# One hybrid decoder layer on one core: the small matmuls of the head turns gathered into fewer groups

## The reference, cut to what matters

```python
q = (rms_norm(c_q) @ w_uq);  kv = (rms_norm(c_kv) @ w_ukv)      # 16 heads, 128 + 64 and 128 + 128 wide
s = (q_nope @ k_nope.T + q_rope @ k_rope.T) * scale             # causal mask, softmax
mla_out = softmax(s) @ v
st = associative_scan(a, B u);   y = Re(C st) + D u             # state-space branch, per group
ssm_out = glu(gelu(y) @ w_glu)
h = layer_norm(alpha * h + (g_ssm * ssm_out + g_mla * mla_out) @ w_out)
h = layer_norm(alpha * h + (silu(h @ w_gate) * (h @ w_up)) @ w_down)
```

## Time and profile before

| what | value |
|---|---|
| median of three runs | 1333.01 us |
| the profiled execution's own time | 1332.76 us |
| its span in the profile | 1330.6 us |
| PE busy | 1320.0 us |
| PE weight loads busy | 1249.1 us |
| DVE busy | 835.4 us |
| ACT busy | 648.7 us |
| granted TensorE clock, mean | 1.00 of full speed |

### The profile page before, as it was taken

How to read it: one execution, slowest core, us unless ns; L and a number is a source line. 1 busy time by engine, 2 the same in 40 slices (tenths; PEclk the granted TensorE clock), 3 DMA queues, 4 the chain that set the end, 5 groups by cost and what they waited for, 6 DMA issues and landing times.

```text
span 1330.6 us, 28260 instructions
## 1 busy us (share of the span) xinstructions
PE 1320.0 (99%) x11052; PEld 1249.1 (94%) x11052; DVE 835.4 (63%) x1232; ACT 648.7 (49%) x910; POOL 23.1 (2%) x50
## 2 busy tenths in 40 slices
PE   9999999999999999999999999999999999999998
PEld 8999999999999998879999999999999998888896
DVE  6787868687786776577555655555555555545545
ACT  5566556474656454365444444444444453434332
POOL 0022000000001000000000000000000000000000
PEclk9999999999999999999999999999999999999999
DMA  8656545545476775754656666666666676556562
GB/s 287 206 190 191 161 157 159 154 141 183 135 192 184 250 246 197 241 169 149 200 190 190 191 195 194 191 190 197 195 190 192 215 236 193 191 173 216 175 207 98
DMA packets 79774, 253.21 MB, mean 190 GB/s; under 512 B 16544, under 2 KB 17504, under 8 KB 79584
## 3 DMA queue, kind: packets, MB, share of 16 engines
q1 hardware_dynamic: 78304, 251.69, 59.8%
q0 software_dynamic: 1408, 0.63, 0.2%
HBM read 248.08 MB, written 2.10 MB: 188 GB/s over the span
## 4 chain that ended last, share of the span: by engine, by line
PE 96%; DVE 2%; ACT 1%; DMA 1%; issue 0%; SPq 0%; DVEq 0%
PE ps L895 22%; PE ps L896 22%; PE ps L897 22%; PE ps L907 9%; PE ps L908 9%; PE ps L909 9%; PE ps L1103 1%; DVE wlo L477 1%; PE ps L1122 1%; PE ps L1099 1%; DMA xrow<-x 0%; PE ps L1034 0%; PE ps L1075 0%; PE ps L1048 0%; PE ps L1056 0%; DVE sqsum L1484 0%
## 5 line engine op out<-in xcount | busy, mean ns | idle before, releaser
L477 DVE TENSOR_TENSOR wlo<-raw,whi 128x1024 fp32r<-128x1024 f32 x450 | 546.8, 1223 | 334.1 <-ACT whi L521 332.1
L521 ACT ACTIVATE whi<-raw 128x1024 fp32r<-128x1024 f32 x450 | 476.6, 1061 | 543.0 <-PE ps L897 340.1
L895 PE MATMUL ps<-hT,whi 128*128 128x256 f32 x1376 | 378.4, 275 | 0.0
L896 PE MATMUL ps<-hT,whi 128*128 128x256 f32 x1376 | 378.4, 275 | 0.0
L897 PE MATMUL ps<-hT,wlo 128*128 128x256 f32 x1376 | 378.4, 275 | 0.0
L895 PEld LDWEIGHTS ps<-hT,whi 128*128 128x128 f32 x1376 | 258.3, 188 | 0.0
L896 PEld LDWEIGHTS ps<-hT,whi 128*128 128x128 f32 x1376 | 258.3, 188 | 0.0
L897 PEld LDWEIGHTS ps<-hT,wlo 128*128 128x128 f32 x1376 | 258.3, 188 | 0.0
L895 PE MATMUL ps<-xT,whi 128*128 128x256 f32 x784 | 221.6, 283 | 0.8 <-DVE wlo L477 0.7
L897 PE MATMUL ps<-xT,wlo 128*128 128x256 f32 x784 | 216.4, 276 | 0.0
L896 PE MATMUL ps<-xT,whi 128*128 128x256 f32 x784 | 216.3, 276 | 0.0
(11 more groups left out here) (274 smaller groups left out, 1482.3 us busy)
## 6 DMA issues: line engine op xcount, KB each, us to landing
raw<-slabs SPq DMA_DIRECT2D x450, 512.0 KB, 4.2
xrow<-x SPq DMA_DIRECT2D x4, 512.0 KB, 6.8
rows<-x SPq DMA_DIRECT2D x4, 512.0 KB, 6.1
gb<-ln_rows SPq DMA_DIRECT2D x4, 512.0 KB, 7.1
eraw<-slabs SPq DMA_DIRECT2D x4, 512.0 KB, 6.3
gb<-ln_rows SPq DMA_DIRECT2D x1, 2048.0 KB, 8.6
out<-rows SPq DMA_DIRECT2D x8, 256.0 KB, 2.6
yb<-u SPq DMA_DIRECT2D x32, 24.0 KB, 3.1
```

What stands on the lines that cost most here:

```text
L477: unit.tensor_tensor(wlo[:, s, :], raw[:, s, :], whi[:, s, :].bitcast(F32), ALU.subtract).then_inc(done, 1 + empty_after)
L521: nc.scalar.activation(whi[:, s, :], raw[:, s, :], ACT.Copy).then_inc(hi_ready, 1 + empty + first)
L895: mm(ps[:, bank, 0:TOK], hi, src[:, kt, 0, :], start=(first and n == 0), stop=False)
L896: mm(ps[:, bank, 0:TOK], hi, src[:, kt, 1, :], start=False, stop=False)
```

## The change

The same instructions are issued, in another order on three engines:

- PE: `weight_turns` goes from behind slab 1 to behind slab 4, directly ahead of `kernels`. `values(0)` goes from behind n = 3 to behind n = 5, where `turn_probs(1)` follows it. `score_pair(1)`, `odd_kernel_parts` and `y_product` all stand behind n = 7, after `values(1)`. `turn_probs(2)` is behind n = 9, `values(2)` and `turn_probs(3)` behind n = 12, `values(3)` behind n = 14. In `score_pair(1)` the plain part comes first and the rotary part last; the signals `scores` of heads 2 and 3 come from the rotary part. The waits in each step stay as they were.
- ACT: `weights_out` goes behind `hp(7)`; `copy_pt` stands at n = 2, 5, 9, 12 and `exps` at n = 0, 3, 7, 9.
- DVE: `head_out(1)`, `head_out(2)`, `head_out(3)`, `softmax_max(2)` and `normalise(2)` change their places between the low parts.

No queue of SP or POOL is changed.

```diff
--- before.py
+++ after.py
@@ -715,14 +715,14 @@
                 base()
                 latent(0, qT, 2)
                 latent(0, qT, 3)
-                weights_out(0)
-                weights_out(1)
                 latent(2, kT, 0)
                 latent(2, kT, 1)
                 hp(6)
                 latent(2, kT, 2)
                 latent(2, kT, 3)
                 hp(7)
+                weights_out(0)
+                weights_out(1)
                 kernel_out()
                 hp(8)
                 trig(i, 0)
@@ -735,10 +735,10 @@
                     if n % 2 == 1:
                         tanh_gate(n // 2)
                     hp(12 + n)
-                    if n % 3 == 0 and n < 12:
-                        exps(n // 3)
-                    if n % 3 == 2 and n < 12:
-                        copy_pt(n // 3)
+                    if n in (2, 5, 9, 12):
+                        copy_pt((2, 5, 9, 12).index(n))
+                    if n in (0, 3, 7, 9):
+                        exps((0, 3, 7, 9).index(n))
                     if last and n == 11:
                         gelu(0, UT - 2)
                     if last and n in (11, 12, 13):
@@ -1094,15 +1094,34 @@
                         pe.wait_ge(max_ready, i * 4 + 1)
                         pe.wait_ge(rotated, i + 2)
                     blocks_ = ((0, 0, P), (1, P, 2 * P))
-                    for q, c0, n in blocks_:
+
+                    def rotated_part(h, q, c0, n):
+                        return mm(ps[:, SCORE[h], c0:c0 + n], qr[half_of(h % 2), p, q * P:(q + 1) * P], zT[half_of(h % 2), 8 + h % 2, 0:n],
+                                  start=(p == 0 and q == 0), stop=(p == 1 and q == 1))
+
+                    def plain_part(h, q, c0, n):
+                        return mm(ps[:, SCORE[h], c0:c0 + n], qT[:, h, q * P:(q + 1) * P], kT[:, h, 0:n],
+                                  start=(p == 1 and q == 0), stop=(p == 0 and q == 1))
+
+                    def rotated_parts():
+                        for q, c0, n in blocks_:
+                            for h in range(2 * p, 2 * p + 2):
+                                ins = rotated_part(h, q, c0, n)
+                                if p == 1 and q == 1:
+                                    ins.then_inc(scores, 1)
+
+                    def plain_parts():
                         for h in range(2 * p, 2 * p + 2):
-                            mm(ps[:, SCORE[h], c0:c0 + n], qr[half_of(h % 2), p, q * P:(q + 1) * P], zT[half_of(h % 2), 8 + h % 2, 0:n],
-                               start=(q == 0), stop=False)
-                    for h in range(2 * p, 2 * p + 2):
-                        for q, c0, n in blocks_:
-                            ins = mm(ps[:, SCORE[h], c0:c0 + n], qT[:, h, q * P:(q + 1) * P], kT[:, h, 0:n],
-                                     start=False, stop=(q == 1))
-                        ins.then_inc(scores, 1)
+                            for q, c0, n in blocks_:
+                                ins = plain_part(h, q, c0, n)
+                            if p == 0:
+                                ins.then_inc(scores, 1)
+                    if p == 0:
+                        rotated_parts()
+                        plain_parts()
+                    else:
+                        plain_parts()
+                        rotated_parts()
 
                 def turn_probs(h):
 
@@ -1137,10 +1156,10 @@
                 pe.wait_ge(c_lo, 8)
                 latent_tiles(0, 0, 2, 0)
                 latent_tiles(1, 1, 2, 0)
-                weight_turns()
                 latent_tiles(2, 2, 2, CT)
                 latent_tiles(3, 3, 2, CT)
                 latent_tiles(4, 4, 2, 0, extra=1)
+                weight_turns()
                 kernels()
 
                 pe.wait_ge(o_read, i * 4 + 1)
@@ -1155,16 +1174,23 @@
                 score_pair(0)
                 for n in range(16):
                     gate_half(n)
-                    if n % 3 == 2 and n < 12:
-                        turn_probs(n // 3)
-                        if n == 5:
-                            score_pair(1)
-                    if n % 3 == 0 and 0 < n < 13:
-                        values(n // 3 - 1)
-                    if n == 6:
+                    if n == 2:
+                        turn_probs(0)
+                    if n == 5:
+                        values(0)
+                        turn_probs(1)
+                    if n == 7:
+                        values(1)
+                        score_pair(1)
                         odd_kernel_parts()
-                    if n == 7:
                         y_product()
+                    if n == 9:
+                        turn_probs(2)
+                    if n == 12:
+                        values(2)
+                        turn_probs(3)
+                    if n == 14:
+                        values(3)
 
 
             for half in (0, 1):
@@ -1712,22 +1738,22 @@
                 head_out(0)
                 turn_forward()
                 head_low(i, 16)
+                head_out(1)
+                head_low(i, 17)
                 softmax_max(2)
-                head_low(i, 17)
-                normalise(2)
                 head_low(i, 18)
                 y_out()
-                head_out(1)
+                normalise(2)
                 head_low(i, 19)
                 softmax_max(3)
                 head_low(i, 20)
                 normalise(3)
-                head_out(2)
                 head_low(i, 21)
                 head_low(i, 22)
+                head_low(i, 23)
+                head_out(2)
+                head_low(i, 24)
                 head_out(3)
-                head_low(i, 23)
-                head_low(i, 24)
                 head_low(i, 25)
             st.leave(HG, DVE_HEAD_STEPS)
```

## The result

The changed kernel takes **1337.22 us** (median of 7 runs, 1336.08 to 1337.73) where the kernel before took 1332.86 beside it: ratio 1.003, 95% interval 1.0021 to 1.0039. It is slower by 2.8 to 5.2 us; 1333.4 was forecast, and the result is outside the range. The profiled execution took 1336.08, the least of the seven; its span is 1333.9, 3.3 more than before.

The account below looks back on a forecast made before the run. PE's own instruction times were taken as the bound. Savings of 3.6 us against waits of 1.5, 1.8 and 0.85 gave +0.5 us, 1333.5 on the median, stated as 1333.4; range 1331.4 to 1335.4.

Parts of the forecast that it names:

- part 1: PE's weight turns placed directly ahead of the kernels: one return to folds and one leaving saved, 0.23 us a turn.
- by how little: Opening question: DVE and ACT now keep up with PE without a gap, so how small is their reserve; no size.
- Wait 1: Behind n = 7, PE's `y_product` waits for PE's own last odd matmul: 0.37 us a turn, 1.5 us in all.
- lower side: Low bound of PE's wait for itself: waiting out the last odd matmul alone costs 0.2 us.
- upper side: High bound of PE's wait for itself, from signal answers 0.31 and 0.15 plus weight load 0.05: 0.50 us more.
- Wait 2: At slab 13 (n = 5), PE arrives before DVE ends the low part: 0.45 us a turn, 1.8 us in all.
- wait 3: At the GLU's start, later `values(3)` delays DVE's `head_out(3)`, slab 25 and `yT` parts: 0.85 us, once.
- Group: Small steps joined behind n = 7: 5.08 us, with head 1's transposes 5.47 for 6.05 before, saving 0.58 a turn.
- joins of values with turns: Values placed beside turns save one return and entry: 0.05 us at n = 5 and 0.05 at n = 12.
- (c): Side cost on PE: after each small group the next eight or so folds are a little slow, 0.05 us.
- rival of slab 4: Slower rival: DVE's low part comes late for the next turn's slab 4, costing 4 us, 1337.4; chance 0.06.
- claim on SP's gathers: In the last turn, SP's gathers queue behind low part 23, which DVE now writes earlier; no cost counted.

Follow-up runs that it names:

- first values alone: Kernel before, with only `values(0)` moved from behind n = 3 to behind n = 5: 1334.86 us, ratio 1.0016.
- The fastest kernel: Changed kernel with base copies later, values(0) at n=3, values(3) at n=13, even parts before PE's self-wait, low part 20 and copy_pt(3) earlier: 1330.18 us.
- the repetition: The changed kernel measured once more, unaltered, beside the kernel before: 1337.20 us (five runs), ratio 1.0033.
- turns a slab earlier: The fastest kernel (1330.18 us) with PE's weight turns one slab ahead of the kernels, giving up that join: 1331.24 us, ratio 0.9982.

## Why the prediction was wrong

- **The step that failed is the pricing of part 1 without a wait.** It said "Saved: 0.23 a turn", looked at the moved `weights_out` on ACT, and found nothing. It never asked what the weight turns' 0.7 us at their old place had been hiding. Each kernel that moves them and leaves `base` where it is has the wait (0.61 a turn, 2.5 us); those that move `base` too have not. The opening gave the rule ("by how little" ACT keeps up), and it was applied to DVE at slab 13 and to `yT`, but not to the evictions at slab 2. The row that would have told it is ACT's third query tile of before: it starts at 191.07, where slab 1's last fold stands at 190.94, so that without the weight turns PE would want the bank at 191.05. The prediction's own sign of being wrong in kind, PE waiting at a slab other than 13, came true at slab 2.
- Wait 1 was over-sized: 0.37 forecast, 0.23 by the step in the group, 0.27 by the run without it. The lower side was nearer. By the formula that the Trainium skill ("TensorE: Matmul & The Clock Gate", Single matmul latency) gives for a single bf16 matmul on the full array, 64 columns take an estimated 0.19; the wait in the trace is just above it. The upper side was also added up 0.05 too high: 0.31 + 0.15 + 0.05 is the step itself, 0.46 more than the 0.05 between neighbours.
- Wait 2 and wait 3 were right in place and mechanism and nearly in size: 0.41 for 0.45 a turn, 0.83 for 0.85. In part this is luck, since two parts of the terms were off and cancel: PE starts 0.05 after the low part ends and not 0.17, and then loses 0.11 on the load, which I had left out.
- The savings were right. Group: 241.12 - 235.92 = 5.20 to the first fold, some 5.36 with the slow return, for 5.08 and a wait: less the measured 0.27, 5.09. Weight turns: 0.23 for 0.23. The joins of values with turns gave 0.05 at n = 12, and 0.02 to 0.03 in the run of the first values alone, for 0.05 each. The fastest kernel, with no wait left, has 0.87 to 0.90 for 0.86.
- The sum: -3.6 + 0.9 + 1.6 + 0.8 + 2.5 = +2.2 us; the profiled execution shows +3.3, the medians +4.4 (2.8 to 5.2). Nearly all of the 1.1 up to the profiled execution is in the trace. Folds behind a wait are slow as in (c), which no term had: from `values(3)` to the next weight turns the third turn takes 357.96 - 340.79 = 17.17 us, and 16.54 with the base copies later, so the query tile costs 0.63 and not 0.61; the three slabs up to slab 13 take 8.76 for 8.31 without a wait, 0.45 and not 0.41; and PE's own wait is 0.27. That is 0.1 a turn, some 0.4 in all; 0.5 is the pause of the second turn (last section), and 0.1 stands behind the sixth tile. What the medians have over the profiled executions, about 1.1 us here and in the repetition, no trace shows; it is within the interval, and stays open.
- The rival of slab 4 did not come, though its 1337.4 is nearest to the measured time: DVE writes its low part at 194.93 to 196.15, PE wants it at 197.77, 1.6 spare where 0.96 was worked out. The claim on SP's gathers was wrong, but costs only where `values(3)` comes earlier.
- The range was too narrow because it held only costs of waits I had found. A wait of the same kind, missed, was worth 2.5 us, more than the 2.0 from the forecast to the range's upper end.
- Two slips decide nothing: by the order of the steps four changes of shape go in each turn, not three, and the ends of the terms add up to 1334.6, not 1334.8.

## What to carry to other kernels

When an engine that is busy all the time gives up a small step, list for every step it passes on the way what the other engines finish under its cover, each bank's eviction too, and not only what reads the moved step's result. A moved step and the order of its neighbours on other engines belong in one edit: the same move cost 2.4 us without the four copies' move, and with it made each turn 0.23 shorter. And read the intervals between matmuls: of the four losses, PE's list of waits named one clearly.

## What was not expected of the hardware

The 128 short kernel matmuls normally take 1.207 us from first to last start. In the third and fourth turn of all fourteen profiles they take 1.206 to 1.209; in the first two they are sometimes interrupted. PE's timeline of the changed kernel, second turn, about the pause:

```profile
202.02 0.20 PE L1034 MATMUL ps<-ca,wpad 64*32 64x48 f32 x1
202.46 0.32 PE L1034 MATMUL ps<-ca,wpad 64*32 64x48 f32 x11 [0.24 <-issue]
```

"Issue" means that no signal held it. First to last start in the second turn, us:

| kernels | second turn |
|---|---|
| turns directly ahead of the kernels (eleven) | 1.69, 1.21, 1.21, 2.05, 1.98, 1.78, 1.32, 1.21, 1.21, 1.21, 1.97 |
| a slab or more between (before, first values alone, turns a slab earlier) | 1.21, 1.21, 1.21 |

In the first turn all are longer, 1.30 to 1.95 in the joined kernels and 1.28, 1.40, 1.41 in the others. With the turns directly ahead the run of short instructions is longer, and the pause comes in six of eleven; three profiles without it are too few to call that shown. On the mean of the eleven it is 0.3 us in the second turn. Whether PE's instructions arrive late there was not tried.

PE waiting for its own last matmul's signal costs 0.23 to 0.27 us here, with 64-column matmuls; a few independent matmuls ahead of the wait hide it.
